# A hybrid RWKV-7 / block-sparse attention layer on one core: the chunk solve spread over four quadrants of TensorE

## What is computed

```python
def step(state, inp):
    r_t, w_t, k_t, v_t, a_t, b_t = inp
    sa = jnp.einsum('bhij,bhj->bhi', state, a_t)
    state = (state * w_t[:, :, None, :] + sa[..., None] * b_t[:, :, None, :]
             + v_t[..., None] * k_t[:, :, None, :])
    y_t = jnp.einsum('bhij,bhj->bhi', state, r_t)
    return state, y_t
```

## Time and profile before

| | us |
|---|---|
| runs of the kernel | 1058.74, 1058.33, 1058.32 |
| median | 1058.33 |
| span of the profiled execution | 1055.6 |
| PE busy | 1014.7 (96%), 8574 matmul records |
| DVE busy | 534.4 (51%) |
| ACT busy | 312.3 (30%) |
| POOL busy | 131.4 (12%) |

### The profile page before, as it was taken

The page is one execution under the profiler, slowest core; times in us unless marked ns, Lnnn a source line. Parts: engine busy times, 40 slices in busy tenths (PEclk is TensorE's granted clock), DMA queues, the critical chain, the costliest instruction groups (busy, mean ns, idle before and its releaser), DMA issues.

```text
span 1055.6 us, 19485 instructions
## 1 busy us (share of the span) xinstructions
PE 1014.7 (96%) x8574; PEld 659.2 (62%) x8574; DVE 534.4 (51%) x815; ACT 312.3 (30%) x536; POOL 131.4 (12%) x152
## 2 busy tenths in 40 slices
PE   8999999999898989999999999999999999999998
PEld 6777899998895678778788443344444443444343
DVE  4568842255546876575665433344333333433354
ACT  4467742033236751231333121111111111111110
POOL 0000000374974500000000100000000000000000
PEclk9999999999999999999999999999999999999999
DMA  9632021000004057466488899999999999999994
GB/s 389 236 116 112 3 81 43 12 5 5 4 4 161 2 186 270 135 224 227 187 368 330 327 409 419 426 427 427 426 427 427 427 425 427 426 428 418 415 415 161
DMA packets 42981, 273.34 MB, mean 259 GB/s; under 512 B 8032, under 2 KB 8176, under 8 KB 28688
## 3 DMA queue, kind: packets, MB, share of 16 engines
q1 hardware_dynamic: 39488, 264.42, 62.1%
q0 software_dynamic: 2400, 4.28, 1.2%
q10 hardware_dynamic: 1008, 3.38, 0.9%
HBM read 272.06 MB, written 4.19 MB: 262 GB/s over the span
## 4 chain that ended last, share of the span: by engine, by line
PE 82%; DMA 8%; DVE 6%; ACT 2%; issue 1%; SPq 0%; DVEq 0%; POOLq 0%; ACTq 0%
PE banks L1722 29%; PE banks L2251 18%; PE banks L2265 9%; DMA w_qkv<-in_w 4%; DMA w_tok<-in_w 4%; PE banks L2289 2%; PE banks L1881 2%; PE banks L2290 2%; PE banks L2257 2%; PE banks L1883 2%; PE banks L1896 1%; PE banks L2237 1%; ACT xT L929 1%; DVE ring L1342 1%; PE banks L1946 1%
## 5 line engine op out<-in xcount | busy, mean ns | idle before, releaser
L1601 DVE TENSOR_TENSOR hid<-banks,silu_a 64x512 f32<-64x512 f32 x32 | 22.2, 693 | 197.9 <-ACT silu_a L934 197.9
L2265 PE MATMUL banks<-w_ring,hidT 128*64 128x512 f32 x512 | 116.8, 598 | 1.1 <-ACT hidT L938 1.1
L1588 DVE SCALAR_TENSOR_TENSOR mod<-banks,row_weight,mod 64x512 f32<-64x512 f32 x64 | 47.9, 748 | 70.3 <-PE banks L2265 69.3
L2251 PE MATMUL banks<-w_tok,xT 128*64 128x512 f32 x176 | 78.3, 596 | 1.8 <-DMA w_ring<-in_w 1.8
L934 ACT ACTIVATE silu_a<-banks 64x512 f32<-64x512 f32 x32 | 18.9, 591 | 206.4 <-PE banks L2252 206.4
L2252 PE MATMUL banks<-w_tok,xT 128*64 128x512 f32 x176 | 79.6, 606 | 0.0
L2252 PE MATMUL banks<-w_ring,xT 128*64 128x512 f32 x176 | 78.3, 596 | 0.0
L1595 DVE TENSOR_TENSOR x<-x,banks 128x1024 f32<-128x1024 f32 x60 | 71.8, 1219 | 12.6 <-PE banks L2290 12.2
L2265 PEld LDWEIGHTS banks<-w_ring,hidT 128*64 128x64 f32 x512 | 34.3, 136 | 67.0 <-issue 65.7
L2251 PE MATMUL banks<-w_ab,xT 128*64 128x512 f32 x160 | 72.4, 606 | 3.8 <-DMA w_tok<-in_w 3.8
L1722 PE MATMUL banks<-x_r,ring_r 128*128 128x512 f32 x192 | 74.8, 390 | 0.0
(11 more groups left out here) (392 smaller groups left out, 2301.6 us busy)
## 6 DMA issues: line engine op xcount, KB each, us to landing
w_ring<-in_w SPq DMA_DIRECT2D x42, 2048.0 KB, 25.5
w_tok<-in_w SPq DMA_DIRECT2D x16, 2048.0 KB, 26.2
ada_buf<-in_w_ada SPq DMA_DIRECT2D x64, 256.0 KB, 3.6
w_ab<-in_w SPq DMA_DIRECT2D x8, 2048.0 KB, 25.9
w_qkv<-in_w SPq DMA_DIRECT2D x7, 2048.0 KB, 29.6
w_tok<-in_w SPq DMA_DIRECT2D x24, 512.0 KB, 16.6
w_ring<-in_w SPq DMA_DIRECT2D x24, 512.0 KB, 17.1
w_ring<-in_w SPq DMA_DIRECT2D x10, 1024.0 KB, 14.6
```

The lines of the kernel that those rows point to most:

```text
L1588: dve.scalar_tensor_tensor(dst[:, 512 * n:512 * n + 512], bank[5][SLOTS * n:SLOTS * n + SLOTS, :], weight_of(e), gate2[:, n, :], ALU.mult, ...
L1601: dve.tensor_tensor(hid[:, :], bank[3][SLOTS:P, :], silu_a[:, :], ALU.mult).then_inc(hid_v, 1)
L2251: pe.matmul(bank[2][0:SLOTS, :], rows, w1_of(k), start=(k == 0), stop=(k == KT - 1))
L2265: mm = pe.matmul(bank[5][SLOTS * n:SLOTS * n + SLOTS, :], hidT[:, k, :], w2[:, k, 512 * n:512 * n + 512], start=(k == 0), stop=(k == 3))
```

## The change

The four steps of a level stay, with other placements. For each group the inverse of chunk c is kept on the partitions of chunk c, and its transpose (and the inner product `PP`) on the partitions of the other chunk, in one tile `MAT` of 512 columns. Thus nm, m5, wu and the state step find operands in both row halves and write both column halves: four quadrants, with results that come from row half 0 in one bank and from row half 1 in the other (`of_rows`). In detail:

- t0 makes the transpose and, by a product with the identity, a copy on the other partitions: 16 matmuls for a group instead of 8. n0 masks both with one instruction of 512 columns over two banks; m0 is gone.
- x writes to the other chunk's partitions, in columns 256 to 511 of `b_`, and waits for n0 instead of `tt`; p writes into `a_`, likewise on the other chunk's partitions.
- nm1 to nm4 have the same 16 matmuls for a group; m5 makes both forms, 16 instead of 8.
- wu has the same 16. q is merged into gh: 32 matmuls for a group behind the one wait on `wu`, and q's wait on g is gone; so `queries_added` now comes behind matmuls that are issued before VectorE's g.
- ScalarE's copies of m5 grow from 256 to 512 columns, and those of nm and wu read 256 columns from each of two banks.

```diff
-        MM_EVENTS = ["ab", "t0", "x"] + LEVELS + ["wu", "gh", "q"]
-        V_EVENTS = ["me", "mo", "tt", "n0", "m0", "p1", "p2", "p3", "p4", "p5", "g", "q"]
+        MM_EVENTS = ["ab", "t0", "x"] + LEVELS + ["wu", "gh"]
+        V_EVENTS = ["me", "mo", "tt", "n0", "p1", "p2", "p3", "p4", "p5", "g", "q"]
...
+                            src, dst = banks[k][:, :, 0:256], (WU if ev == "wu" else MAT)[k].rearrange("p s h n -> p s (h n)")
...
-                            ins = dve.tensor_tensor(INV[k], f4(a_[:, 0:256]), bc4("level0"), ALU.mult)
-                        elif ev == "m0":
-                            dve.wait_ge(solve_v[k], v_at(half, "tt"))
-                            ins = dve.tensor_tensor(INVT[k], FORMS[k][:, 0], bc4("level0_t"), ALU.mult)
+                            ins = dve.tensor_tensor(MAT[k], banks[k][:, :, 0:256].rearrange("p s (h n) -> p s h n", h=4),
...
+                    if ev == "t0":
+                        for c, rows, other in halves_of:
+                            pe.matmul(of_rows[c][rows, at], FORMS[k][rows, 0, i, :], const("eye2")[rows, :], start=True, stop=True)
+                        for c, rows, other in halves_of:
+                            mm = pe.matmul(of_rows[c][other, at], const("eye2")[rows, :], FORMS[k][rows, 0, i, :], start=True, stop=True)
+                    elif ev == "x":
+                        for c, rows, other in halves_of:
+                            mm = pe.matmul(b_[other, far], FORMS[k][rows, 1, i, :], V_[c], start=True, stop=True)
+                    elif ev[0] == "p":
+                        for c, rows, other in halves_of:
+                            mm = pe.matmul(a_[other, far], FORMS[k][rows, 0, i, :], MAT[k][rows, c, i, :], start=True, stop=True)
+                    elif ev[0] in "nm":
+                        for c, rows, other in halves_of:
+                            inv_t, prod = MAT[k][other, c, i, :], PP[k][other, i, :]
+                            pe.matmul(of_rows[c][rows, at], *((inv_t, prod) if ev[0] == "n" else (prod, inv_t)), start=True, stop=True)
+                        for c, rows, other in halves_of:
+                            mm = pe.matmul(of_rows[c][other, at], PP[k][other, i, :], MAT[k][other, c, i, :], start=True, stop=True)
+                    elif ev == "wu":
+                        for c, rows, other in halves_of:
+                            pe.matmul(of_rows[c][rows, at], MAT[k][rows, c, i, :], Ah[c], start=True, stop=True)
+                        for c, rows, other in halves_of:
+                            mm = pe.matmul(of_rows[1 - c][rows, at], MAT[k][other, c, i, :], XX[k][other, i, :], start=True, stop=True)
+                    else:
+                        for c, rows, other in halves_of:
+                            pe.matmul(a_[rows, at], WU[k][rows, c, i, :], Bt[c], start=True, stop=True)
+                        for c, rows, other in halves_of:
+                            pe.matmul(b_[other, at], Bt[c], WU[k][rows, 1 - c, i, :], start=True, stop=False)
+                        for c, rows, other in halves_of:
+                            pe.matmul(a_[rows, far], WU[k][rows, c, i, :], FORMS[k][rows, 2, i, :], start=True, stop=True)
+                        for c, rows, other in halves_of:
+                            mm = pe.matmul(b_[other, at], Kt_[c], V_[c], start=False, stop=True)
```

More of the change, by code:

```diff
@@ L53, in shape_constants @@
         if n == 0:
-            parts["level0_t"] = below(col, row) + parts["eye2"]
+            below_t = below(col, row) + parts["eye2"]
+            lower_half = r < CH
+            parts["level0"] = np.concatenate([np.where(lower_half, parts["level0"], below_t), np.where(lower_half, below_t, parts["level0"])], 1)
     parts["head_ones"] = same * 1.0
@@ L173, in hybrid_layer @@
         FORMS = [flat[:, 3072 * k:3072 * k + 1024].rearrange("p (f h n) -> p f h n", f=4, h=4) for k in range(NG)]
-        INV, INVT = ([group_part(k, at, 256) for k in range(NG)] for at in (1024, 1280))
-        PP, XX, WU, HH = ([group_part(k, at, n) for k in range(NG)] for at, n in ((1536, 256), (1792, 256), (2048, 512), (2560, 256)))
-        GG, QQ = PP, INV
+        MAT, WU = ([flat[:, 3072 * k + at:3072 * k + at + 512].rearrange("p (s h n) -> p s h n", s=2, h=4) for k in range(NG)] for at in (1024, 2048))
+        PP, XX, HH, QQ = ([group_part(k, at, 256) for k in range(NG)] for at in (1536, 1792, 2560, 1024))
+        GG = PP
         HH_OF = [flat[:, 6144 * i:6144 * i + 6144].rearrange("p (g n) -> p g n", g=2)[:, :, 2560:2816] for i in range(2)]
@@ L1270, in queries_added @@
                 a_, sc, g = bank[2 * k], 2 * half + k // 2, k % 2
-                dve.wait_ge(solve_mm[k], mm_at(half, "q"))
+                dve.wait_ge(solve_mm[k], mm_at(half, "gh"))
                 for c in range(2):
@@ L1865, in solve_step @@
                 a_, b_ = bank[2 * k], bank[2 * k + 1]
+                of_rows = (a_, b_)
                 sc = 2 * half + k // 2
@@ L1892, in solve_step @@
-                    for c in range(2):
-                        rows, other = slice(CH * c, CH * c + CH), slice(CH * (1 - c), CH * (1 - c) + CH)
-                        V_, Bt, Kt_ = (tokm[rows, sc, ct, q, hc] for q in range(3))
-                        if ev[0] == "n":
-                            mm = pe.matmul(a_[rows, 256 + CH * i:256 + CH * i + CH], PP[k][rows, i, :], INVT[k][rows, i, :], start=True, stop=True)
-                        elif ev == "wu":
-                            mm = pe.matmul(b_[rows, P * i + HD:P * i + P], INVT[k][rows, i, :], XX[k][rows, i, :], start=True, stop=True)
-                        elif ev == "gh":
-                            mm = pe.matmul(b_[other, at], Bt, WU[k][rows, i, HD:P], start=True, stop=False)
@@ L1901, in solve_step @@
-                    if ev == "gh":
-                        for c in range(2):
-                            rows, other = slice(CH * c, CH * c + CH), slice(CH * (1 - c), CH * (1 - c) + CH)
-                            mm = pe.matmul(b_[other, at], tokm[rows, sc, ct, 2, hc], tokm[rows, sc, ct, 0, hc], start=False, stop=True)
+                    hc, at, far = slice(HD * odd, HD * odd + HD), slice(CH * i, CH * i + CH), slice(256 + CH * i, 256 + CH * i + CH)
+                    halves_of = [(c, slice(CH * c, CH * c + CH), slice(CH * (1 - c), CH * (1 - c) + CH)) for c in range(2)]
@@ new lines, in solve_step @@
+                    V_, Bt, Kt_, Ah = ([tokm[rows, sc, ct, q, hc] for _, rows, _ in halves_of] for q in range(4))
+                    if ev == "t0":
[29 more added lines that the diff above has]
+                            mm = pe.matmul(b_[other, at], Kt_[c], V_[c], start=False, stop=True)
@@ L1933, in outputs @@
                             i = 2 * j + odd
-                            pe.matmul(dst[odd], WU[k][rows, i, HD:P], FORMS[k][rows, 2, i, :], start=True, stop=False)
+                            pe.matmul(dst[odd], WU[k][rows, 1 - n % 2, i, :], FORMS[k][rows, 2, i, :], start=True, stop=False)
                         for odd in range(2):
@@ L1954, in _ @@
                     for k in range(NG):
[L1955 removed]
+                        if ev == "t0":
                             pe.wait_ge(solve_v[k], v_at(half, "tt"))
[L1957 removed]
+                            if half == 0 and k < NG - 1:
                                 between(bank[2 * k][:, 256:256 + P], 6)
[L1959 removed]
+                        elif ev in ("x", "p1"):
                             pe.wait_ge(solve_v[k], v_at(half, "n0"))
[L1961 removed]
                         elif ev[0] == "p":
                             pe.wait_ge(solve_a[k], a_at(half, f"nm{int(ev[1]) - 1}"))
[L1964 to L1966 removed]
                         elif ev[0] in "nm":
                             pe.wait_ge(solve_v[k], v_at(half, "p" + ev[-1]))
+                            if ev == "nm1":
+                                pe.wait_ge(solve_a[k], a_at(half, "x"))
                         elif ev == "wu":
                             pe.wait_ge(solve_a[k], a_at(half, "m5"))
[L1971 removed]
+                        else:
                             pe.wait_ge(solve_a[k], a_at(half, "wu"))
[L1973 to L1974 removed]
                         solve_step(half, k, ev)
```

55 lines of the change are left out of this document (7 added, 48 removed).

## The result

The changed kernel is **slower**: 1073.3 us (median; 1072.8 to 1074.2) against 1058.3, a ratio of 1.0149 with a 95% interval from 1.0132 to 1.0166. The forecast was 1060.2, its range 1053 to 1067. The sign was the likelier one, the size was outside.

A forecast was written before the change was run, and what follows sets the result against it. PE, busy 96%, was taken as bound by instruction supply, 3.6 us per 256. First half +2.0 us, middle -0.5, second half with m0's lost stall and clock: +1.7 at the solve's end; +1.7 to +2 gave 1060.2 us, range 1053 to 1067.

The forecast's parts named there:

- Blocks of 256: Both halves of the solve: PE's instructions come in blocks of 256, one per 3.6 us, with some 18 issue stops.
- Rival A: Solve: instruction supply does not bind, so work by quadrants counts; some -20 us, 1038 us; chance 0.10.
- VectorE's order: End of first half: four additions of queries now stand behind g; gh ends at 252.3, chain(0,1) starts at 255.2.
- The middle, -0.5: Between the halves: a block in hand gives back 0.5 us, so the second half's t0 starts at +1.5.
- m0 and n0: Second half: m0's 2.2 us stall and 1.7 us clock loss go; n0 costs 0.75 us each for 0.42.
- After the solve everything follows PE: Behind the solve: no transfer is at its limit before the experts; turn_qk follows the last outputs near 321 us.
- Rival C, the clock: Inside the solve: idle lowers the clock; three blocks with p cost up to 1.5 us each, +4: 1064 us; chance 0.10.

The follow-up runs named there:

- run 11: Changed kernel with six identity products of 256 columns on one quadrant of TensorE ahead of the chain of states in either half: 1060.4 us.
- run 4: Kernel before with 32 columns instead of 64 in the products of levels 2 to 4, part of the inverse not computed: 1056.9 us.
- 12: Kernel before without the fourth head's products in levels 2 to 4 and the last p, part not computed: 1051.7 us.
- 13: Kernel before with m0 right behind the forms and wu's two products merged into one of 128 columns: 1054.7 us, ratio 0.9986.
- 14: Kernel before with m0 behind the forms, wu merged, g and q merged, and VectorE's order changed at the halves' ends: 1054.6 us, ratio 0.9977.
- run 1: Changed kernel with six dense identity products of 256 columns on TensorE in the wait ahead of the chain in either half: 1060.5 us, ratio 1.0043.
- run 2: Changed kernel with VectorE doing the first two groups' sums and first state before g of groups 2 and 3: 1058.6 us, ratio 1.0031.
- 5: Kernel before with VectorE copying the first state four more times, holding back the first chain: 1056.9 us, ratio 1.0012.
- 10: Changed kernel with VectorE's new order at the halves' ends and two dense products ahead of the chain: 1056.6 us, ratio 1.0014.

## Why the prediction was wrong in size and right in sign

- **Blocks of 256.** Right in mechanism: stops named issue all through both halves, 20 for some 18 forecast, two packets more, nm at 14.6 ns a pair. The period was 3.8 in the first half, for 3.6 forecast, and 3.6 in the second: the end of gh came at 253.89 for 252.3, of which the late start of t0 (0.4) is a part. The same instructions took 1.7 us less in run 11's profile (43.2 for 44.9), so some of this is chance. In the second half, from t0 to the end of gh, 43.1 us were forecast and 43.9 measured. The Trainium skill's page "Runtime: NRT & Kernel Launch", section Instruction fetch mechanics, has it that fetching is hidden behind execution. Rival A is what that would give; the 20 stops, 128 pairs apart, disagree. Runs 4, 12, 13 and 14 are of the kernel before, whose levels have no stops, and don't decide it.
- **VectorE's order.** Right: 2.9 us were forecast between the end of gh and chain(0,1), 2.6 measured. At the end of the second half it was 1.6.
- **The middle, -0.5.** Wrong: +3.5. The step "the stretch begins with a block in hand, so I give back 0.5" took the clock as given. With the clock held, in run 1's profile, chain(0,1) to t0 took 13.2 us for the 13.7 of before: the -0.5 that was forecast.
- **m0 and n0.** n0 with 512 columns took 0.68 us, less than the 0.75 taken. The lost wait of 2.2 us and the clock's dip after it did go.
- **After the solve everything follows PE.** Right in order, but not in pace: turn_qk came at 333.7, not 321.
- **Rival C, the clock** is the term that was mis-sized: "three of them, +4: 1064", chance 0.10. I looked for idle inside the levels, priced a fall by blocks of nm and p, and let it be short, as the one dip of before. The failed step is that price and place: the sum itself had nothing for the clock behind the ends of the halves. It fell where a new wait of mine stood (2.6 and 1.6 us) behind a half full of stops, and ahead of 13.7 and 14.4 us in which PE was 100% busy with 64x64 products; there half the clock cost 3.5, 6.5 and then 2.3 us: 12.3. Run 1 gave back 11.2 by the ratios, and in its profile chain(0,1) to t0, chain(1,0) to turn_qk and turn_qk to the merge took 13.2, 8.0 and 57.9 us again. The time without it, 1073.3 - 12.3 = 1061.0, is near the forecast's 1060.2, in part by luck: the first half and VectorE's wait gave 3.3 with the late start, for 2.0 forecast, and 0.8 of it was made up behind the merge.

Not settled: which idle, exactly, brings the clock down. Runs 2, 5 and 10 fell in some executions and not in others of the same kernel, and of each only one was profiled.

## What to carry to other kernels

Where PE's stops named issue lie 256 instructions apart, count instructions, not columns: products with the same weights belong in one matmul of more columns, and quadrants buy nothing. Test supply in a kernel that has the stops: in one without them an instruction can have its price from another cause. Price a new wait of TensorE by what stands behind it at half clock, not by its own length, and fill it with products that nobody reads, no longer than the wait. Before moving an operation ahead, look at what queues behind it in its new place, and how long it takes there.

## What the runs showed of the hardware

- TensorE, at 100% busy by the profile for nearly all of it, stayed at half clock for 13.7 us behind the first half, and from about 318 to 338.6 us behind the second.
- PE got 256 instructions of the solve in 3.5 to 4.0 us, whatever work they held (2.1 to 3.1 us of it, 16 blocks of the changed kernel's profile).
- On two quadrants, 64x64 and 64x32 products both came at 29 ns a pair of records (64 pairs of p in 1.87 us in the kernel before, 62 in 1.81 us in run 4).
- One quadrant kept the clock up as the whole array did (runs 11 and 1: 1060.4 and 1060.5 us, clock 1.00 in both profiles from 254 to 270 us).
- The same mask of 128x256 from SBUF on VectorE took 0.42 us and 1.52 us in one profile, with GpSimd at work beside both; the cause was not tested.
- The same kernel ran at two mean clocks: 0.997 with 1057.0 us and 0.985 with 1067.2 us in run 2.
